# Stick-breaking attention stage: the next scores, the value products and a four-block unit's weights in another order

## The reference, cut to what matters

```python
def stick_breaking_attention(q, k, v):
    for blk in range(s // SB_BLOCK):             # 4 query blocks of 128
        logits = q_blk @ k[:k_end].T * scale
        strict = query position > key position
        log_beta = log_sigmoid(logits)
        log_keep = where(strict, log_sigmoid(-logits), 0)
        log_tail = cumsum(log_keep, reverse=True) - log_keep
        weights = where(strict, exp(log_beta + log_tail), 0)
        outs.append(weights @ v[:k_end])
...
mixed = concatenate([rms_norm(oa) * g_a, rms_norm(ob) * g_b]) @ w_out
```

## Time and profile before

| | |
|---|---|
| runs of the kernel before | 1840.78, 1843.7, 1844.63 us; median 1843.7 |
| profiled execution | 1839.02 us, span 1837.3 us |
| TensorE busy | 1789.6 us, 97% of the span |
| VectorE busy | 1099.8 us, 60% |
| ScalarE busy | 728.3 us, 40% |
| mean granted TensorE clock | 0.997 |

### The profile page before, as it was taken

The page is one execution under the profiler, slowest core; times in us unless marked ns, Lnnn a source line. Parts: engine busy times, 40 slices in busy tenths (PEclk is TensorE's granted clock), DMA queues, the critical chain, the costliest instruction groups (busy, mean ns, idle before and its releaser), DMA issues.

```text
span 1837.3 us, 23078 instructions
## 1 busy us (share of the span) xinstructions
PE 1789.6 (97%) x8616; PEld 1443.7 (79%) x8616; DVE 1099.8 (60%) x1609; ACT 728.3 (40%) x1023; POOL 40.6 (2%) x78
## 2 busy tenths in 40 slices
PE   7999989999999999999999999999999999999998
PEld 6787645788888888878888888889766888888886
DVE  6978755655556335765676774245567466776423
ACT  5322654344443323443434343233356344444322
POOL 4010000000000000000000000000000000000000
PEclk9999999999999999999999999999999999999999
DMA  9694111332223223222223322323401223322221
GB/s 350 220 358 139 47 52 57 104 103 91 91 91 107 87 96 99 92 70 92 92 91 106 100 91 80 109 82 108 161 24 47 69 92 102 103 91 91 92 103 69
DMA packets 149083, 195.32 MB, mean 106 GB/s; under 512 B 3646, under 2 KB 133000, under 8 KB 146332
## 3 DMA queue, kind: packets, MB, share of 16 engines
q1 hardware_dynamic: 141272, 155.28, 25.8%
q0 software_dynamic: 7600, 39.13, 5.7%
q10 hardware_dynamic: 148, 0.05, 0.0%
HBM read 189.15 MB, written 5.29 MB: 106 GB/s over the span
## 4 chain that ended last, share of the span: by engine, by line
PE 87%; DVE 7%; ACT 3%; DMA 2%; issue 1%; POOL 0%; DVEq 0%; ACTq 0%; POOLq 0%
PE bank L786 20%; PE bank L787 20%; PE bank L788 20%; PE bank L849 3%; PE bank L851 2%; PE bank L850 2%; PE bank L1410 2%; PE bank L1411 2%; PE bank L1412 2%; PE bank L932 2%; PE bank L968 2%; DMA ada_stage<-in_w_ada 1%; PE bank L949 1%; PE bank L829 1%; PE bank L830 1%
## 5 line engine op out<-in xcount | busy, mean ns | idle before, releaser
L1867 DVE TENSOR_TENSOR w_lo<-w_stage,w_hi 128x2048 fp32r<-128x2048 f32 (+3 forms) x135 | 296.7, 2198 | 444.1 <-ACT w_hi L1438 443.9
L786 PE MATMUL bank<-act_hi,w_hi 128*128 128x512 f32 x1232 | 483.2, 392 | 4.1 <-DVE act_lo L2229 2.8
L787 PE MATMUL bank<-act_lo,w_hi 128*128 128x512 f32 x1232 | 480.8, 390 | 0.0
L788 PE MATMUL bank<-act_hi,w_lo 128*128 128x512 f32 x1232 | 480.8, 390 | 0.0
L1438 ACT ACTIVATE w_hi<-w_stage 128x2048 fp32r<-128x2048 f32 (+3 forms) x137 | 251.7, 1837 | 459.0 <-PE bank L788 334.1
L786 PEld LDWEIGHTS bank<-act_hi,w_hi 128*128 128x128 f32 x1232 | 231.9, 188 | 55.7 <-issue 3.7
L788 PEld LDWEIGHTS bank<-act_hi,w_lo 128*128 128x128 f32 x1232 | 231.8, 188 | 48.0
L787 PEld LDWEIGHTS bank<-act_lo,w_hi 128*128 128x128 f32 x1232 | 231.8, 188 | 47.9 <-issue 0.5
L788 PE MATMUL bank<-mid_hi,w_lo 128*128 128x512 f32 x352 | 137.1, 390 | 0.0
L787 PE MATMUL bank<-mid_lo,w_hi 128*128 128x512 f32 x352 | 137.1, 390 | 0.0
L786 PE MATMUL bank<-mid_hi,w_hi 128*128 128x512 f32 x352 | 137.1, 390 | 0.0
(11 more groups left out here) (412 smaller groups left out, 2631.0 us busy)
## 6 DMA issues: line engine op xcount, KB each, us to landing
ada_stage<-in_w_ada POOLq DMA_DIRECT2D x24, 1024.0 KB, 7.2
w_stage<-in_w_up SPq DMA_DIRECT2D x22, 1024.0 KB, 5.0
w_stage<-in_a_ffn_in SPq DMA_DIRECT2D x22, 1024.0 KB, 5.0
w_stage<-in_b_ffn_in SPq DMA_DIRECT2D x22, 1024.0 KB, 5.1
w_stage<-in_w_in SPq DMA_DIRECT2D x10, 1024.0 KB, 7.1
w_stage<-in_b_ffn_out SPq DMA_DIRECT2D x10, 1024.0 KB, 5.0
w_stage<-in_w_down SPq DMA_DIRECT2D x8, 1024.0 KB, 4.9
w_stage<-in_a_ffn_out SPq DMA_DIRECT2D x8, 1024.0 KB, 4.9
```

The lines of the kernel that those rows point to most:

```text
L786: pe.matmul(dst, wh, mh, start=start and k == 0, stop=False)
L787: pe.matmul(dst, wh, ml, start=False, stop=False)
L788: last = pe.matmul(dst, wl, mh, start=False, stop=stop and k == nk - 1)
L1867: dve.tensor_tensor(w_lo[slot][:, 0:n], raw[:, 0:n], w_hi[slot][:, 0:n].bitcast(FP32), ALU.subtract).then_inc(w_ready, 1)
```

## The change

Two lists get another order; no instruction is added or taken away, and the data are the same.

On TensorE `sb_qk(u + 2)` moves up: it comes right behind `sb_tail_sum(u)`, and so ahead of `mem_half(1, 1)` (u = 1) and of `sb_values` (u = 4, 8, 12). For a four-block unit (u = 3, 7, 11) it comes ahead of `sb_tail_sum(u)` itself. On ScalarE `sb_weigh` of a four-block unit (units 3, 7 and 11, in steps 5, 9 and 13) comes behind `softplus(u)` of that step, no longer ahead of it. The waits inside the functions stay as they are.

```diff
@@ TensorE @@
+                four = u % 4 == 3
+                if four and u + 2 < SB_UNITS:
+                    sb_qk(u + 2)
                 sb_tail_sum(u)
+                if not four and u + 2 < SB_UNITS:
+                    sb_qk(u + 2)
                 if u == 1:
                     pe.wait_ge(out_saved, 4)
                     mem_half(1, 1)
...
                 if u and u % 4 == 0:
                     sb_values(u // 4 - 1)
-                if u + 2 < SB_UNITS:
-                    sb_qk(u + 2)
@@ ScalarE @@
             for u in range(SB_UNITS + 2):
-                if u >= 2:
+                four = (u - 2) % 4 == 3
+                if u >= 2 and not four:
                     sb_weigh(u - 2)
                 if u < SB_UNITS:
                     softplus(sb_clip(u), sb_clamped, sb_exped, sb_logged, u + 1)
+                if u >= 2 and four:
+                    sb_weigh(u - 2)
```

## The result

The changed kernel takes 1846.58 us (median of 15 runs, 1843.64 to 1850.29), the kernel before in the same comparison 1840.83 us (15 runs, 1838.11 to 1847.95). The ratio is 1.0025, 95% interval 1.0016 to 1.0033: 4.6 us slower, 2.9 to 6.1.

A forecast was written before the change was run, and what follows sets the result against it. TensorE, busy 97% of the span, was taken as the bound, so stage changes count one to one. Terms -0.9 + 1.9 + 2.2 + 2.4 = 5.6 us on 1843.7 gave 1849.3 us, range 1844.0 to 1852.5.

The forecast's parts named there:

- 2.4 of clock: TensorE idle 4.2 and 3.3 us at second and third boundary: two falls to 1.2 GHz, 1.2 us each, 2.4 us lost.
- The order: All three boundaries without the clock term: the new instruction order makes the stage end 3.2 us later.
- First boundary: Steps 1 to 6: early scores bring Exp(6) from 249.58 to 248.65 us, 0.9 us gained.
- Second and third boundary: Steps 7 to 10 and 11 to 14: weights of units 7 and 11 run late, losing 1.9 and 2.2 us.
- One reading ahead of the sum: Clip's waits for scores, 9.3 us in all before, said to come back at units 9, 10 and 13, 14.
- the chain of scores, values and save: Exp(6) waits for scores, values, save and weights one after the other; the early scores' gain is given back at the save.
- The number of falls: Two falls of the granted clock, near 264 and 284 us; chance 0.45.
- the factor of 1.7: Six matmuls took 1.34 us at the lower clock, 0.80 at full; so 3.4 us low cost at most 1.4 us.
- The early scores: Rival: clip's waits for scores vanish and nothing replaces them, 9.3 us less, 1834.4 us; chance 0.04.
- No fall: Rival: clock doesn't fall, only 3.2 us lost, 1846.9 us; chance 0.25.
- The loss did reach the end: Answers the rival that the loss doesn't reach the end, or the boundaries cancel: 1843.7 us; chance 0.06.
- DMA: Later loads for w_out and memory-value store, about 1.3 us late, stay covered by over 60 us behind the stage.

The follow-up runs named there:

- the filler: Changed kernel plus matmuls nobody reads: 768 columns behind tail sums of units 7, 8 and 12, 256 behind unit 11: 1844.62 us, ratio 1.0010.
- the two filled kernels: Changed kernel, and TensorE's order alone, each with unread matmuls added in TensorE's idle stretches: 1844.62 us and 1837.16 us.
- TensorE's order alone: Kernel before with only TensorE's new list, ScalarE's list as before: 1839.74 us, ratio 0.9991.
- ScalarE's order alone: Kernel before with only ScalarE's new list: 1852.58 us, ratio 1.0054; with unread matmuls ahead of the first three groups of values, 1849.27 us.
- the kernel with the later save: Changed kernel with each pair's save one step later on ScalarE, behind the softplus of units 6, 10 and 14: 1846.1 us, ratio 1.0022.

## Why the prediction was right

**The sum.** Forecast -0.9, +1.9, +2.2 and 2.4 of clock: 5.6 us. The stage shows 5.90, the whole runs 4.6 (2.9 to 6.1). By the filler the stage splits into order (22.78 - 24.11 = -1.33, 19.70 - 17.97 = +1.73, 18.92 - 16.95 = +1.97, together 2.35 with the 0.02 us behind them) and clock (3.55). The order was forecast at 3.2 us, 0.85 too much, and the clock at 2.4, 1.15 too little. That the sum comes within 0.3 us of the stage is in part luck: the two errors cancel.

**First boundary.** Right in its steps, 0.4 us too little. Counted from the first Exp, unit 3's tail sum was to start at 239.9 - 225.47 = 14.4 us and started at 238.37 - 224.18 = 14.2; Exp(6) was to start at 23.2 and started at 22.8. Each step was a little shorter than summed, none was wrong.

**Second and third boundary.** The two boundaries were put at 1.9 and 2.2 us and lost 1.7 and 2.0. That the late weights and not TensorE's order are this loss is shown by the two filled kernels, with the clock at 1.00 in both: the late weights are all that the changed kernel has beyond TensorE's order alone, and they cost 22.78 - 22.77 = 0.0, 19.70 - 17.65 = 2.05 and 18.92 - 16.73 = 2.19 us. The first of these was forecast too: there the weights aren't held. One reading ahead of the sum was wrong: that the waits for scores come back at units 9 and 13. In the kernel before only the clips of units 3, 5, 6, 10 and 14 wait for scores; in the changed one those of 4, 6, 10 and 14 do, and at 6, 10 and 14 they wait longer than before. The sum itself didn't use that reading. The save ahead of the next Exp is shown as a holder too, but as the smaller one: taking it out gave 2.0 us in the changed kernel, clock included. The forecast named the chain of scores, values and save as if the save closed it; the values close it by themselves one unit later.

**The clock.** The number of falls came true, and the second came near 284 us as forecast. The first came at another place than was argued. The forecast put it near 264 us (262.7 if counted from this execution's first Exp), behind the wait for the late weights of unit 7, and counted the 4.2 us of idle time around unit 8's tail sum as one stretch. The clock was at 0.50 from 259.7 us on, behind the first 1.88 us of it and 1.6 us before those weights started. It was a wait hardly longer than the 1.84 us that the forecast took as harmless. TensorE's order makes this wait and fall by itself; what the late weights add is that scores and values stand behind it, still at the lower clock.

The term was mis-sized: 1.2 us each was taken, with 1.4 as the bound, and they cost 1.95 and 1.60. One cause is the factor of 1.7 from the earlier trace rows. The values of this stage, wholly at the lower level in ScalarE's order alone, took 4.53 us against 2.37, a factor of 1.9:

```profile
251.35 4.53 PE L1036 MATMUL bank<-sb_w,vb_tok 128*64 128x512 f32 x16 [2.61 <-ACT sb_w L1701]
```

By 1.9 the 3.4 us of a fall cost 1.6 us, which is what the second measured. The other cause is the low time, 6.8 us at the first fall (259.7 to 266.6 us), not 3.4. Of it 4.1 us lie over the scores and the first two thirds of the values, and by the same factor that makes 2.0 us. Both are estimates, and both meet what the filler gave.

**The rivals.** The early scores didn't pay in full: Exp(6) stood behind save and weights and started 2.1 us after its clip had ended. "No fall" would be the filled kernel, 2.35 us of stage; two profiles of the changed kernel, each with both falls, rule it out. The loss did reach the end: behind Exp(14) nothing was won back (14.34 against 14.35).

**DMA.** The chain behind the stage has no DMA in it before or after, so nothing on it came to wait for the later loads, as expected.

## What to carry to other kernels

Before an instruction is moved behind another on an engine that works in order, list who waits for it on the other engines, here the next scores, which need its bank; take the change apart by engine list, since one half can be worth something (1.9 us of the stage here, with the clock held up) and the other cost more than that (4.2 us). Here the wait for a big product was better placed behind the next small step of the chain than ahead of it, by 1.8 to 2.0 us of the stage. A stall of TensorE can cost twice where work on the path follows it: add the lower clock to its price, for short stalls as well, or put work into it. And compare the parts of a forecast, not only its sum: here two errors of about 1 us hid each other.

## What the runs showed of the hardware

In the changed kernel the granted clock stood at 0.50 from 259.7 to 266.6 us, 6.8 us and twice as long as in each of the two falls that the forecast was read from. Matmuls of about 1.5 us that nobody reads, in three of its idle stretches, and of 0.6 us in a fourth, kept it at 1.00 and made the stage 3.55 us shorter. The Trainium skill says in its page TensorE: Matmul & The Clock Gate, "HAM oscillation — how this bites in real kernels", that idle gaps between bursts let the next burst start at the lower clock. The traces agree for the long gaps: in two profiles of the changed kernel the scores and values behind both ran at 0.50, all but the first 0.4 us of the scores at the second gap and the end of the values at both.

Equal waits aren't always followed by an equal clock. A wait of 1.9 us ahead of the same tail sum, behind the same instructions, was followed by a fall in both profiles of ScalarE's order alone (with and without filler), and by none in both profiles of the kernel before. The wait of 1.88 us ahead of unit 8's tail sum was followed by a fall in both profiles of the changed kernel and in that of TensorE's order alone, and by none in the kernel with the later save. What differs isn't known and wasn't followed up, so how a fall behind a wait of this length comes about stays open. The scatter of whole runs, up to 10 us for the kernel before, is the clock at least in part. Both its profiles have the same stage, and the second stood at the lower level for 8.8 us more outside it. By the factor of 1.9 that is about 4.2 us, an estimate, of the 5.2 us between them (1839.02 and 1844.21 us). Why a fall outside the stage is there in one execution and not in the next stays open too.
